# Two-block transformer in fp32 on one core: weight slots beside the ring in the expert stages, and a 31-tap convolution shared among the engines

## What is computed

```python
# first block, per layer: a mixer, then a mixture of experts
x = x + mixer(rmsnorm(x, norm_mix))
x = x + ec_moe(rmsnorm(x, norm_ffn))
# ec_moe: 16 experts, each takes its 32 best tokens
gates, idx = top_k(softmax(h @ w_router).T, 32)
xs = h[idx]                                   # (16, 32, 1024)
y = (silu(xs @ w_gate[e]) * (xs @ w_up[e])) @ w_down[e]    # 1024 -> 512 -> 1024
out[idx] += gates * y

# second block: half-step FFNs around a mixer; the mixer of its first layer:
u = rmsnorm(h) @ w_in
attn = window_attention(q, k, v, sinks, bias by distance)   # 8 heads, window 128
glu = u[a] * sigmoid(u[b])                    # 512 channels
c = silu(layernorm(causal_depthwise_conv(glu, conv_w (31 taps), conv_b)))
h = h + concat([attn, c]) @ w_out
```

## Time and profile before

| | |
|---|---|
| median of 3 runs | 1791.35 us (1790.51 to 1792.87) |
| the profiled execution's own time | 1795.65 us |
| its span, first to last instruction | 1793.8 us |
| mean granted TensorE clock (1.00 is 2.4 GHz) | 0.92 |
| busy: PE, PEld, DVE, ACT, POOL | 84%, 67%, 48%, 33%, 1% |
| HBM read | 407.02 MB, 227 GB/s over the span |

### The profile page before, as it was taken

How to read it: one execution, slowest core, us unless ns; L and a number is a source line. 1 busy time by engine, 2 the same in 40 slices (tenths; PEclk the granted TensorE clock), 3 DMA queues, 4 the chain that set the end, 5 groups by cost and what they waited for, 6 DMA issues and landing times.

```text
span 1793.8 us, 26383 instructions
## 1 busy us (share of the span) xinstructions
PE 1498.2 (84%) x10708; PEld 1210.5 (67%) x10708; DVE 866.0 (48%) x1560; ACT 593.0 (33%) x955; POOL 25.7 (1%) x33
## 2 busy tenths in 40 slices
PE   7896765668868566499998869999899998889997
PEld 6764422247654222299997548999899997679997
DVE  5663210137732111265553985555655555465555
ACT  5451100024711000154441254444444431554442
POOL 0000000001000000000000000000000000000000
PEclk9997987879969888899998979999999998989999
DMA  9522999994119999965554414555455552345520
GB/s 405 230 94 108 429 426 429 428 429 188 52 62 428 426 429 429 428 248 186 187 188 156 168 33 155 188 188 187 152 195 188 187 217 87 148 156 189 189 90 24
DMA packets 31022, 409.21 MB, mean 228 GB/s; under 512 B 3376, under 2 KB 5424, under 8 KB 6368
## 3 DMA queue, kind: packets, MB, share of 16 engines
q1 hardware_dynamic: 28496, 404.85, 56.8%
q10 hardware_dynamic: 2448, 3.24, 0.6%
HBM read 407.02 MB, written 1.06 MB: 227 GB/s over the span
## 4 chain that ended last, share of the span: by engine, by line
PE 58%; DMA 18%; issue 12%; DVE 8%; ACT 3%; POOL 0%; SPq 0%; DVEq 0%; ACTq 0%; POOLq 0%
DMA ring<-stream 18%; PE bank L1477 7%; PE bank L1478 7%; PE bank L1481 7%; PE bank L1509 7%; PE bank L599 5%; PE bank L1515 3%; PE bank L605 3%; PE bank L1305 2%; PE bank L1750 2%; PE bank L1286 2%; DVE cat L1694 2%; PE bank L579 2%; PE bank L372 2%; PE bank L1609 2%
## 5 line engine op out<-in xcount | busy, mean ns | idle before, releaser
L471 DVE TENSOR_TENSOR unit_lo<-ring,unit_hi 128x1024 fp32r<-128x1024 f32 x324 | 394.9, 1225 | 331.6 <-ACT unit_hi L466 331.3
L466 ACT ACTIVATE unit_hi<-ring 128x1024 fp32r<-128x1024 f32 x324 | 341.5, 1060 | 461.5 <-PE bank L1481 285.5
L1477 PE MATMUL bank<-hT_hi,unit_hi 128*128 128x256 f32 x1408 | 343.1, 282 | 0.1
L1478 PE MATMUL bank<-norm_lo,unit_hi 128*128 128x256 f32 x1408 | 342.2, 281 | 0.0
L1477 PEld LDWEIGHTS bank<-hT_hi,unit_hi 128*128 128x128 f32 x1408 | 266.9, 190 | 3.6 <-DVE norm_lo L410 0.3
L1478 PEld LDWEIGHTS bank<-norm_lo,unit_hi 128*128 128x128 f32 x1408 | 266.3, 189 | 3.1
L1286 PE MATMUL bank<-ring,work 128*32 128x256 f32 x2048 | 147.9, 444 | 88.7 <-DMA ring<-stream 76.0
L1481 PE MATMUL bank<-hT_hi,unit_lo 128*128 128x256 f32 x1408 | 194.2, 279 | 0.0
L1286 PEld LDWEIGHTS bank<-ring,work 128*32 128x32 f32 x2048 | 71.4, 124 | 165.8 <-DMA ring<-stream 99.3
L1481 PEld LDWEIGHTS bank<-hT_hi,unit_lo 128*128 128x128 f32 x1408 | 178.1, 188 | 0.0
L1509 PE MATMUL bank<-unit_hi,act_hi 128*128 128x512 f32 x336 | 132.5, 394 | 0.0
(11 more groups left out here) (248 smaller groups left out, 1820.0 us busy)
## 6 DMA issues: line engine op xcount, KB each, us to landing
ring<-stream SPq DMA_DIRECT2D x191, 2048.0 KB, 14.1
work<-spread ACTq DMA_DIRECT2D x2, 1024.0 KB, 6.7
par<-params SPq DMA_DIRECT2D x1, 1455.5 KB, 17.2
x<-x_in SPq DMA_DIRECT2D x1, 1024.0 KB, 4.9
out<-x SPq DMA_DIRECT2D x2, 512.0 KB, 2.7
con<-consts SPq DMA_DIRECT2D x1, 640.0 KB, 6.0
cat<-final_rows ACTq DMA_DIRECT2D x1, 512.0 KB, 3.4
work<-final_rows ACTq DMA_DIRECT2D x1, 512.0 KB, 5.3
```

The lines of the kernel that those rows point to most:

```text
L466: nc.scalar.activation(high_buf(name, u), raw_unit(name, u), ACT.Copy).then_inc(hi_done, 1)
L471: low = nc.vector.tensor_tensor(low_buf(name, u), raw_unit(name, u), high_buf(name, u).bitcast(F32), ALU.subtract)
L1477: nc.tensor.matmul(out, high[:, k, :], hT_hi[:, k, :], start=(k == 0), stop=False)
L1478: nc.tensor.matmul(out, high[:, k, :], norm_lo[:, k, :], start=False, stop=False)
```

## The change

**Expert stages.** `AHEAD = 3`: the three slots of expert 2 of each expert stage leave the stream (now 45 slots a stage instead of 48) and come from a second DRAM array, `ahead`. SP issues their DMAs in its own queue, behind the refills that fill the ring for the stage and behind a wait on `x_ready`: two into the space of `work` columns 0 to 8191, the third into the space of `hT` once the router matmuls have read it. `hsel` is gone: each group gathers its own tokens with 128 columns of `pick` (`gather_pe`), group 1 to 3 at their start, behind `scatter_added`; ScalarE and DVE scale them into `hcur`. GpSimd now copies 2 x 128 columns of `pick` and `pcur`. The 512 KB row load for the norm behind `moe1`, which ScalarE issued before that stage, is issued in its group 0, behind expert 2.

```diff
-("moe0", 3 * E) ... ("moe1", 3 * E)
+AHEAD = 3
+("moe0", 3 * E - AHEAD) ... ("moe1", 3 * E - AHEAD)
+        ahead_buf = [region(0, (SLOT,)), region(SLOT, (SLOT,)),
+                     nc.alloc_sbuf_tensor_at("ahead2", [P, SLOT], F32, offset=hT_base)]
+            def load_ahead(l):
+                sp.wait_ge(x_ready, l + 1)
+                for i in range(AHEAD):
+                    if i == AHEAD - 1:
+                        sp.wait_ge(route_pe, 5 * l + 1)
+                    sp.dma_start(ahead_buf[i][:, :], ahead[AHEAD * l + i, :, :]).then_inc(ahead_in[i], 16)
+            marks = [START["moe0"] + RING, START["moe1"] + RING]
+            refills(RING, marks[0])
+            load_ahead(0)
+            refills(marks[0], marks[1])
+            load_ahead(1)
+            refills(marks[1], N_SLOTS)
+        def gather_pe(pe, chosen_at):
+            for k in range(KD):
+                for t in range(NT):
+                    mm = nc.tensor.matmul(bank[k // 4][:, (k % 4) * P:(k % 4 + 1) * P], xn[:, t, k * P:(k + 1) * P],
+                                          chosen_at(t), start=(t == 0), stop=(t == NT - 1))
+                if k % 4 == 3:
+                    mm.then_inc(gathered, 1)
             def others():
-                for k in range(KD):
...
-                        mm = nc.tensor.matmul(bank[k % 4][:, P:4 * P], xn[:, t, k * P:(k + 1) * P], pick[:, t, P:4 * P],
...
             group(0, True)
             with pe.Fori(1, E // GRP) as g:
                 pe.wait_ge(staged, 3 * l + g)
+                pe.wait_ge(scatter_added, 4 * l + g)
+                gather_pe(pe, lambda t: pick_g[:, t, :])
+                pe.wait_ge(hcur_out[0], 4 * l + 1 + g)
+                pe.wait_ge(hcur_out[1], 4 * l + 1 + g)
                 group(g, False)
+                    if first and e == 2 and l == 1:
+                        act.dma_start(W[:, 0:D], bass.AP(tensor=final_rows.tensor, offset=0, ap=[[0, P], [1, D]]))\
+                           .then_inc(final_in, 16)
```

```diff
-        TAPS = [(j, 2 * pair + c) for pair in range(2) for j in range(KW) for c in range(2)]
+        VECTOR_TAPS = [(1, j) for j in range(LEAD)]
+        for j in range(KW):
+            VECTOR_TAPS += [(1, LEAD + j)] * (LEAD + j < KW) + [(2, j), (3, j)]
+            def weighted(first, end):
+                for j in range(first, end):
+                    ge(act, pool_tap, j - 4)
+                    src, _, w = tap_parts(0, j)
+                    nc.scalar.activation(products[j % 4], src, ACT.Copy, scale=w).then_inc(product, 1)
+            gate(0)
+            act.wait_ge(spread_ready, 1)
+            act.dma_start(bass.AP(tensor=spread, offset=0, ap=[[P * (SPAN + 1), S_HEADS], [SPAN + 1, P], [1, SPAN]]),
+                          spread_sb.unsqueeze(1).to_broadcast([S_HEADS, P, SPAN])).then_inc(spread_out, 16)
+            act.wait_ge(wide_dve, 1)
+            weighted(1, 7)
+            gate(1)
+            act.wait_ge(spread_out, 16)
+            for t in range(NT):
+                src = bass.AP(tensor=spread, offset=2 * P - 1 - P * t, ap=[[SPAN, P], [P * (SPAN + 1), S_HEADS], [1, T]])
+                act.dma_start(bias_s[:, :, t * T:(t + 1) * T], src).then_inc(rows_in, 16)
+            weighted(7, 14)
+            gate(2)
+            weighted(14, 21)
+            gate(3)
+            weighted(21, KW)
             proj_copy(act, "s_in", 0, lambda c: (uS[:, 0, 0:512], uS[:, 0, 512:768])[c])
-            for h in range(S_HEADS):
-                act.wait_ge(bias_done, h + 1)
...
+        def s_mix_pool(pool):
+            acc = conv_s[0]
+            for j in range(1, KW):
+                pool.wait_ge(product, j)
...
+                tap = nc.gpsimd.tensor_tensor(acc, products[j % 4], acc, ALU.add)
+                tap.then_inc(conv_done if j == KW - 1 else pool_tap, 1)
-            taps(0, 28)
+            taps(0, LEAD)
             gated(2)
             gated(3)
-            taps(28, 84)
+            taps(LEAD, LEAD + COPY_AFTER)
...
-            taps(84, 104)
+            taps(LEAD + COPY_AFTER, LEAD + COPY_AFTER + 6)
             turn_evac(v, 1, "s1")
-            attend_dve(v, "s", lambda i: taps(104 + 5 * i, 109 + 5 * i))
+            v.wait_ge(rows_in, 32)
+            attend_dve(v, "s", lambda i: taps(LEAD + COPY_AFTER + 6 + 8 * i, LEAD + COPY_AFTER + 14 + 8 * i), norm_conv)
+            split_proj(v, 1, "s_out", evac=conv_low)
-            step(v, nc.vector.tensor_tensor(ct, ct, pc("lng").unsqueeze(1).to_broadcast([P, NT, 512]), ALU.mult))
-            nc.vector.tensor_tensor(ct, ct, pc("lnb").unsqueeze(1).to_broadcast([P, NT, 512]), ALU.add)\
```

More of the change, by code:

```diff
@@ L63, with build @@
 SPAN = 512
-def build(nc, stream, params, consts, buckets, final_rows, x_in, out):
+LEAD = 14
+COPY_AFTER = 50
+def build(nc, stream, ahead, params, consts, buckets, final_rows, x_in, out):
     ctx = ExitStack()
@@ L163, in build @@
         staged = sem("staged")
+        ahead_in = [sem(f"ahead_in{i}") for i in range(AHEAD)]
+        ahead_used = sem("ahead_used")
+        gathered = sem("gathered")
+        hcur_out = [sem("hcur_out_act"), sem("hcur_out_dve")]
         expert_gu = sem("expert_gu")
@@ L618, in split_proj @@
                     midway()
-                if name != "a_out" and j >= TURNED_FROM.get(SPLIT_PROJ[name], 0):
-                    split_evac(eng, which, SPLIT_PROJ[name], j)
+                if j >= TURNED_FROM.get(SPLIT_PROJ[name], 0):
+                    if evac is not None:
+                        evac(eng, j)
+                    elif name not in ("a_out", "s_out"):
+                        split_evac(eng, which, SPLIT_PROJ[name], j)
                 if j >= EARLY or name not in STAGE_AFTER.values():
@@ L925, in heads_lo_dve, with attend_dve @@
                                     ALU.subtract).then_inc(cat_low, 1)
-        def attend_dve(v, name, between=None, first=None):
+        def attend_dve(v, name, between=None, last=None, first=None):
             n = PAIRS[name]
@@ L940, in attend_dve @@
                     between(i)
+            if last is not None:
+                last(v)
             heads_lo_dve(v, name, n - 2)
@@ L1278, in group, with weights, spent @@
                 seen = 4 * l + g
+                later = 0 if first else 32 * (g - 1)
                 for e in range(GRP):
-                    na, nb, nd = n0 + 3 * e, n0 + 3 * e + 1, n0 + 3 * e + 2
+                    na, nb, nd = moe_slots(n0, e, first)
+                    kept = first and e == 2
+                    def weights(i, n):
+                        if kept:
+                            pe.wait_ge(ahead_in[i], 16 * (l + 1))
+                            return ahead_buf[i]
+                        pe.wait_ge(slot_in[n % RING], 16 * (n // RING + 1) + later)
+                        return slot(n)
+                    def spent(mm, n):
+                        if kept:
+                            mm.then_inc(ahead_used, 1)
+                        else:
+                            release(mm, n)
                     for half, n in enumerate((na, nb)):
-                        pe.wait_ge(slot_in[n % RING], 16 * (n // RING + 1) + 32 * g)
-                        w = slot(n).rearrange("p (k m c) -> p k m c", k=4, m=2)
+                        w = weights(half, n).rearrange("p (k m c) -> p k m c", k=4, m=2)
                         for kk in range(4):
@@ L1291, in group @@
                         if half == 0:
[L1292 removed]
+                            spent(mm, na)
                         else:
@@ L1360, in group @@
                         act.wait_ge(scattered, seen + 1)
-                    act.wait_ge(slot_used[nd % RING], nd // RING + 1 + 2 * g)
+                    if first and e == 2:
+                        act.wait_ge(ahead_used, AHEAD * (l + 1))
+                    else:
+                        act.wait_ge(slot_used[nd % RING], nd // RING + 1 + (0 if first else 2 * (g - 1)))
                     for i in range(2):
@@ L1434, in group @@
                         v.wait_ge(scattered, seen + 1)
-                    v.wait_ge(slot_used[nd % RING], nd // RING + 1 + 2 * g)
+                    if first and e == 2:
+                        v.wait_ge(ahead_used, AHEAD * (l + 1))
+                    else:
+                        v.wait_ge(slot_used[nd % RING], nd // RING + 1 + (0 if first else 2 * (g - 1)))
                     for i in range(2, 4):
@@ L2190 @@
     out = nc.dram_tensor("out", (T, D), F32, kind="ExternalOutput").ap()
-    build(nc, args["stream"], args["params"], args["consts"], args["buckets"], args["final_rows"], args["x_in"], out)
+    build(nc, args["stream"], args["ahead"], args["params"], args["consts"], args["buckets"], args["final_rows"], args["x_in"], out)
     r = run(nc, [arrays], core_ids=[0]).results[0]
```

319 lines of the change are left out of this document (166 added, 153 removed).

## The result

| | us, median (range, runs) | ratio to before, 95% interval |
|---|---|---|
| before | 1791.68 (1787.61 to 1795.90, 10) | |
| changed | 1797.32 (1792.51 to 1801.75, 10) | 1.0030 (1.0017 to 1.0043) |

One execution of all that are reported here stands far apart, 5099.49 us for a kernel of experiment 5 (the slots alone with 8 unused columns), and is left out of its ratio.

What follows compares the result with a forecast made beforehand. Bounds: the weight stream in expert stages; in stage s, TensorE's channel tiles, then DVE's taps. Profiled 1795.65 - 29.4 + 1.2 - 0.2 - 8.5 = 1758.75 us; by medians 1791.35 - 36.9 = 1754.5 us, range 1750.5 to 1762.5.

Steps and rivals of the forecast that it cites:

- The failed step: Stage s, bias: 6.7 us for the 2 MB row write, again for the reads; back by 992 us, needed by 1024.
- plateau: Expert stages: stretch where the weight stream runs at 426 to 429 GB/s, 4.90 us a slot; to shorten by three slots.
- Expert stages, -29.4, +1.2, -0.2: Three early slots save 14.7 us in each of two stages; moved row load costs 1.2; smaller `con` at start saves 0.2.
- Rivals 2 and 4: Expert stages: stream breaks at group boundary, 2 us each stage, 1758.5, chance 0.08; early slots not early, 1784, chance 0.02.
- Taps, -7.8: Stage s before the heads: 50 DVE taps at 0.40 us behind the last gate, evacuation ending at 1022.1, not 1029.9 us.
- rival 1: Stage s: GpSimd's adds and DVE's taps shut each other out, 10 adds cost 6.1 us, total 1760.6; chance 0.33.
- warmer around the heads: Stage s: TensorE pauses less around the heads, so a warmer clock; 4 us allowed at the range's lower end.
- GpSimd's add, 0.61: Stage s, moved convolution tile: each 128 x 256 add takes 0.61 us; up to about 1.2 us it costs nothing.
- Rival 3: Stage s: GpSimd's add is slow and delays ScalarE's projection copy; at 4 us an add, 63 us, 1818; chance 0.03.
- Heads and norm, -0.7: Stage s, heads through `s_out`: 8 more taps there cost 3.2 us, yet the norm gives 0.7 us beyond the taps' lead.
- stage `s`: Whole stage 8.5 us shorter, most of it from the taps and only 0.7 from the norm.

Runs made afterwards that it cites:

- experiment 5: Unused columns put in SBUF to move the work area's address; on the kernel before with the early slots alone, 8 columns: 1760.06 us, ratio 0.9820.
- the last kernel of experiment 3: Changed kernel with the bias rows written from 128 partitions, and ScalarE's wait and the two reads moved behind gate 3: 1754.25 us, ratio 0.9796.
- experiment 4: On the old bias path kernel: GpSimd's 30 adds replaced by one-column writes, 1756.48 us; or tile 0's taps back on DVE, 1755.18 us.
- old bias path: Changed kernel with the bias going its old way (16 KB write, flip matmuls, ScalarE's copies): 1755.95 us, ratio 0.9799.

## Why the prediction was wrong

**The failed step** is this sentence on the bias: "With as much for the write and again for the reads: 992 us, hidden with 30 us to spare." "As much" was 6.7 us. The earlier trace rows is two reads into 128 partitions. I took its duration for a write of the same bytes out of 8 partitions, in 2 KB rows at odd addresses. The write took 47.45 us, seven times as much, of which the narrow source is 28 (19.7 when wide) and, with the wide source, the odd addresses 12.5 (7.2 when aligned). I gave that cost no upper end, although no row of the kernel before has such a transfer, and no rival held it; the one rival on the slow side was placed at GpSimd.

The Trainium skill has a rule that would have given such a write a price of its own. "SBUF — State Buffer", section "Door 1: The DMA port swizzle", says that a DMA's bandwidth goes by how many of 16 ports its partitions reach. Partitions 0 to 7 reach two by its formula. A sixteenth of the two plateaus' 428 GB/s is 27 GB/s a port, an estimate; two ports give 54 GB/s and 39 us for 2.1 MB. The trace agrees: 50 GB/s while the weights lay almost still. What the runs don't separate is the ports from the number of packets under way, 7.3 with the narrow source, up to all 16 engines with the wide one; the copy from DRAM, with 8 rows as its source, none of them in SBUF, also had 8.5 at most and took 35.94 us.

**The wait's queue.** My own working said "ScalarE's last gate hangs on TensorE". It hangs on all that stands ahead of it on ScalarE, and the change had put there a wait for a DMA. Had I asked what is queued behind `act.wait_ge(spread_out, 16)`, the answer would have been the products and two gates. In the last kernel of experiment 3 these run at 954.97 and 961.88, 13 and 20 us behind the issue of the write at 941.90: that was its cover, not the 47 us up to 1024 that I counted.

Point by point, by the terms of the sum:

- *Expert stages, -29.4, +1.2, -0.2:* right in mechanism. 31.3 us up to the end of `ffn0`, of which 1.4 are its FFN pace. The rest, 29.9, is 1.5 more than the 28.4 forecast, which is within what traces of the same code differ by (in two kernels of experiment 4, which have the same code up to there, the norm behind `moe1` begins at 722.5 and 729.1 us). The slots came when expected, `moe0`'s last long wait ended 14.9 us earlier where I had 14.7, and the plateau did not break; the gather took 3.8 us where I had 6.4. Rivals 2 and 4 fell.
- *Taps, -7.8:* from the last gate to the masks it took 35.2 us before (996.92 to 1032.08), 30.6 with the old bias path (962.87 to 993.46) and 32.4 with the skewed bias repaired (962.29 to 994.67): -4.6 and -2.8. Two things are missing from 7.8. The first is in DVE's own part. That part, up to its evacuation, went from 32.2 to 28.6 us in both, by 3.6 us: the term was mis-sized by **rival 1**, which came true. While GpSimd adds, DVE's taps wait; I had priced it at 6.1 us and measured 4.7. My argument from the earlier trace rows against it didn't hold: the `pow` beside which DVE lost nothing says nothing of an add of 256 columns. The trace agrees on this with the Trainium skill, "SBUF — State Buffer", section "Who interferes with whom"; that an add of 0.73 us costs DVE 0.47 and not the whole is what the row shows. The second thing is TensorE, which I had expected warmer around the heads and which is colder there without the flips: from the evacuation to the masks it took 3.8 us with the skewed bias, 2.9 before, 2.0 with the flips in the changed order.
- *GpSimd's add, 0.61:* 0.73 us, and 0.87 with its semaphores. Rival 3 fell.
- *Heads and norm, -0.7:* +2.8 with the old bias path and +0.8 with the skewed bias repaired (49.9 us from the masks to `s_out`'s first add before, 52.7 and 50.7 there). The working had +3.2 for the 8 taps more and so, by its sum, -3.9 for the norm. The taps are right (19.8 and 23.0 us up to the last normalization, experiment 4). The norm is mis-sized: from there to `s_out`'s first add it took 30.1 us before and 29.7 and 27.7 in these two, so it gives 0.4 to 2.4 us. Why these two differ, with the same code in that stretch, isn't shown.
- *FFN stages:* no term. By the traces an address gave about 1.4 us in each of four stages; `ffn0`'s is in the 31.3 us and the three behind are most of the 4.7.

So without the write's price stage `s` would have given 2 us, not 8.5 (83.1 us from the last gate to `s_out`'s first add in the repaired kernel, 85.1 before), and the faster FFN stages, for which there was no term, nearly made up for that: the kernel with the skewed bias repaired takes 1754.25 us. That this is the number of the forecast is luck, a sum of misses and not a proof of its terms.

## What to carry to other kernels

- A DMA is priced by its source, its destination and its row, not by its bytes. Ask how many partitions it leaves from, how many packets are under way, and at what step its rows lie (528 words were fast here, 513 slow); where no row of the trace has that shape, both ends of its cost belong in the range.
- A wait is priced by what stands behind it in its engine's queue and by when that is due. Here some 25 us hung on whether it stood ahead of two gates or behind them.
- Two engines that share a vector loop over SBUF may wait for each other; give the second one its part in the first one's idle time, or give it none. Here the split won 1 us at most.

## What was unexpected of the hardware

- 2 MB from 8 partitions at rows of 513 words: 47.45 us, in two kernels to the hundredth. From 128 partitions: 19.7 and 16.9. From 128 with rows of 528 words: 7.2, in one execution.
- The address of an area in SBUF sets the pace of the FFN stages: 192.9, 194.3, 194.9 and 196.15 us at 96, 64, 32 and 0 bytes past a multiple of 128. Eight unused columns ahead of the kernel before, and nothing else, give a ratio of 0.9985 (0.9976 to 0.9994).
- The flips, which run beside DVE's taps and end nothing there, keep TensorE's granted clock at 1.00 up to the heads when they end just ahead of them (989.9 us with the old bias path, masks at 993.46); without them it is at 0.50 there. In the kernel before they end at 1024.0 us, and in 1030 to 1033 us the clock is at 0.50 as well.
